# Scores of first and second attention in three fp32r passes, and the last product in column halves

## What is computed

```python
def sliding_window_sink_attention(q, k, v, sinks):          # "first attention"
    ...
    s = jnp.einsum('bnqkgd,bnskd->bnkgqs', qb, kb).astype(jnp.float32) * scale
    ...
    m = jnp.maximum(jnp.max(s, axis=-1, keepdims=True), sink)
    p = jnp.exp(s - m)
...
        sc = jnp.einsum('bqkgd,bskd->bkgqs', qi, ki).astype(jnp.float32) * scale   # windowed_gqa, "second attention"
...
        x = x + jnp.square(jax.nn.relu(h2 @ w_up[l])) @ w_down[l]                  # the last product
    return rms_norm(x, norm_final)
```

## Time and profile before

| | |
|---|---|
| median of 3 runs | 1072.89 us (1072.5 to 1072.98) |
| the profiled execution | 1072.29 us |
| its span, first to last instruction | 1070.5 us |
| mean granted TensorE clock | 0.998 of 2.4 GHz |
| TensorE matmul busy | 1061.8 us, 99% |
| VectorE, ScalarE, GpSimd busy | 797.9, 567.5, 162.4 us |

### The profile page before, as it was taken

One profiled execution on the slowest core, in us unless ns is written; L12 is line 12 of the kernel. 1 busy time (PEld: TensorE's weight loads), 2 busy tenths in 40 slices (PEclk: granted clock), 3 DMA queues, 4 the chain that ended last, 5 costly groups with the idle time before them and its releaser, 6 DMA issues.

```text
span 1070.5 us, 14582 instructions
## 1 busy us (share of the span) xinstructions
PE 1061.8 (99%) x5220; PEld 857.5 (80%) x5220; DVE 797.9 (75%) x1339; ACT 567.5 (53%) x965; POOL 162.4 (15%) x261
## 2 busy tenths in 40 slices
PE   9999999999999999999999999999999999999997
PEld 7787787887777788767778889988888888888886
DVE  7888887867888865376556669975795886796795
ACT  6766766556676544254354437644453443443455
POOL 2000000120665421022134310012000000000003
PEclk9999999999999999999999999999999999999999
DMA  6422232332121233222423235334704503503301
GB/s 232 143 73 89 93 95 92 118 118 89 41 80 40 80 99 107 91 62 77 137 81 99 79 124 152 102 119 146 264 0 142 193 1 118 197 0 114 141 1 79
DMA packets 35960, 109.97 MB, mean 103 GB/s; under 512 B 4016, under 2 KB 9008, under 8 KB 35888
## 3 DMA queue, kind: packets, MB, share of 16 engines
q1 hardware_dynamic: 34880, 106.09, 29.5%
q0 software_dynamic: 576, 2.10, 1.1%
q10 hardware_dynamic: 432, 0.86, 0.2%
HBM read 103.26 MB, written 2.10 MB: 98 GB/s over the span
## 4 chain that ended last, share of the span: by engine, by line
PE 95%; DVE 1%; ACT 1%; SPq 1%; DMA 1%; issue 0%; DVEq 0%; ACTq 0%
PE ps L1139 23%; PE ps L1141 23%; PE ps L1140 23%; PE ps L1076 5%; PE ps L1077 5%; PE ps L1078 5%; PE ps L1229 2%; PE ps L1309 2%; PE ps L1273 2%; PE ps L1095 1%; PE ps L1096 1%; PE ps L1097 1%; SPq L917 1%; PE ps L1303 1%; PE ps L1025 1%; PE ps L1243 1%
## 5 line engine op out<-in xcount | busy, mean ns | idle before, releaser
L1139 PE MATMUL ps<-xgh,wh 128*128 128x512 f32 x783 | 309.9, 396 | 0.8 <-DVE xgl L1796 0.5
L1141 PE MATMUL ps<-xgh,wl 128*128 128x512 f32 x783 | 305.2, 390 | 0.0
L1140 PE MATMUL ps<-xgl,wh 128*128 128x512 f32 x783 | 305.0, 389 | 0.0
L1738 DVE TENSOR_TENSOR wl<-raw,wh 128x1024 fp32r<-128x1024 f32 x144 | 180.6, 1255 | 38.1 <-ACT wh L1349 36.5
L1349 ACT ACTIVATE wh<-raw 128x1024 fp32r<-128x1024 f32 x144 | 150.8, 1050 | 74.9 <-PE ps L1141 53.6
L1139 PEld LDWEIGHTS ps<-xgh,wh 128*128 128x128 f32 x783 | 147.0, 188 | 36.4 <-issue 7.2
L1141 PEld LDWEIGHTS ps<-xgh,wl 128*128 128x128 f32 x783 | 147.0, 188 | 31.4
L1140 PEld LDWEIGHTS ps<-xgl,wh 128*128 128x128 f32 x783 | 147.1, 188 | 29.5 <-issue 0.2
L1554 ACT ACTIVATE Pt<-Pt,stat 128x256 f32<-128x256 f32 (+2 forms) x128 | 64.3, 503 | 89.9 <-DVE stat L2014 34.8
L1076 PE MATMUL ps<-wh,fh 128*128 128x512 f32 x224 | 87.1, 389 | 0.0
L1077 PE MATMUL ps<-wl,fh 128*128 128x512 f32 x224 | 87.1, 389 | 0.0
(11 more groups left out here) (294 smaller groups left out, 1918.2 us busy)
## 6 DMA issues: line engine op xcount, KB each, us to landing
raw<-wst SPq DMA_DIRECT2D x144, 512.0 KB, 3.5
b<-wdn SPq DMA_DIRECT2D x32, 512.0 KB, 6.8
bst<-nbias SPq DMA_DIRECT2D x8, 256.0 KB, 3.5
xtok<-xblk SPq DMA_DIRECT2D x16, 128.0 KB, 2.5
gx<-xT SPq DMA_DIRECT2D x3, 512.0 KB, 6.6
outT<-xtok SPq DMA_DIRECT2D x3, 512.0 KB, 2.6
Vb<-vblk SPq DMA_DIRECT2D x16, 64.0 KB, 2.0
wt<-woc SPq DMA_DIRECT2D x2, 512.0 KB, 4.7
```

Source lines behind the costliest of these rows:

```text
L1139: e.matmul(o, high, a, start=(k == 0), stop=False)
L1140: e.matmul(o, high, b, start=False, stop=False)
L1141: done = e.matmul(o, low, a, start=False, stop=stop)
L1738: e.tensor_tensor(wl_t[:, v % NHL, :], src, f32(wh_t[:, v % NHL, :]), ALU.subtract).then_inc(lo_done, 1)
```

## The change

Scores. `sink_scores` and `window_scores` take the place of the float32 matmul of L1229. Each runs three fp32r passes in place of one float32 matmul. The high parts are ScalarE copies, the low parts VectorE subtractions: of the keys once, of the queries chunk by chunk. The key copies `ke` and `kea` go; in their place the keys' two parts are swapped between the halves of the partitions by four DMAs each (`ksh2`, `ksl2`, `kah2`, `kal2`). The parts of the queries need room and get it where tensors lie that are written later: first attention's in the place of `sgt` (chunks 0 to 3) and of the upper half of `y2h` and `y2l` (chunks 4 to 7), second attention's in the place of `yah` and `yal`. So the first write of `sgt` waits for the 32nd score. `qa` shrinks to two buffers.

Last product. The twelve 512 column matmuls of the last product become 24 of 256 columns, first all of the left column half, into a PSUM bank of its own (6), then the right half. The left half of what bank 1 held is added before; the left half of the last product is added and squared while TensorE is at the right half, and the last square and the last add are 256 columns wide. Its weight units' places are set for the new order.

```diff
@@ class Chunks, downs
             for i in range(8):
-                self.unit_of.append((len(self.units) + i // 2 % 2, 2 * (i // 4) + i % 2))
-            self.units += [(("form", r, "P4", 0), t, t + 5), (("form", r, "P4", 1), t + 2, t + 7)]
+                self.unit_of.append((len(self.units) + (i // 2 if i < 4 else i) % 2, i % 4))
+            self.units += [(("form", r, "P4", 0), t, t + 6), (("form", r, "P4", 1), t + 2, t + 7)]
@@ SyncE, swaps
-                q.wait_ge(qn_done, 1)
-                e.dma_start(ke[1][lo, :], qu[0][hi, :]).then_inc(swap_in, 16)
-                e.dma_start(ke[0][hi, :], qu[0][lo, :]).then_inc(swap_in, 16)
...
+                q.wait_ge(ksh_done, 1)
+                e.dma_start(f32(ksh2[lo, :]), f32(ksh[hi, :])).then_inc(swap_in, 16)
+                e.dma_start(f32(ksh2[hi, :]), f32(ksh[lo, :])).then_inc(swap_in, 16)
+                q.wait_ge(ksl_done, 1)
+                e.dma_start(f32(ksl2[lo, :]), f32(ksl[hi, :])).then_inc(swap_in, 16)
+                e.dma_start(f32(ksl2[hi, :]), f32(ksl[lo, :])).then_inc(swap_in, 16)
...
@@ TensorE
+            def last_down_tile(name, i, v):
...
+                if i == 0:
+                    q.wait_ge(ev_done, ev_no(("up", FINAL, 5)))
+                    q.wait_ge(quarter_done, 1)
+                o = bank[(LAST_BANK, ch.bank[name])[i // 2]][:, 256 * (i // 2):256 * (i // 2) + 256]
+                for k in (2 * (i % 2), 2 * (i % 2) + 1):
...
+                    e.matmul(o, a, wh_t[:, v % NHL, w], start=(k == 0 and i == 0), stop=False, skip_group_check=True)
+                    e.matmul(o, a, wl_t[:, v % NHL, w], start=False, stop=False, skip_group_check=True)
+                    done = e.matmul(o, b, wh_t[:, v % NHL, w], start=False, stop=(k == KH - 1), skip_group_check=True)
...
+            def sink_scores(m, i, a, job):
+
+                g = job["g"]
+                q.wait_ge(q1h_done, 4 * g + a + 1)
+                q.wait_ge(q1l_done, 4 * g + a + 1)
...
+                q.wait_ge(swap_in, 64)
+                q.wait_ge(qn_done, 3 + 4 * g + 2 * job["half"])
+                for n, (own, seen) in enumerate(((q1h[g], (ksh, ksh2)), (q1l[g], (ksh, ksh2)), (q1h[g], (ksl, ksl2)))):
+                    for p, r in ((0, lo), (1, hi)):
+                        done = e.matmul(score_place(m, i + p), own[r, a, blk(job["n"])], seen[p != g][r, keys(job)],
+                                        start=(n == 0), stop=(n == 2))
+                        if n == 2:
+                            done.then_inc(score_done, 1)
+
+            def window_scores(m, i, a, job):
...
@@ ScalarE
+            def sink_key_high():
+                yield sum_tick(0) + 3.8
+                q.wait_ge(qn_done, 1)
+                q.wait_ge(tile_done, A_END)
+                e.activation(ksh, qu[0], ACT.Copy).then_inc(ksh_done, 1)
+
+            def sink_query_highs():
+                for c in range(8):
+                    yield sum_tick(c + 1) + (2.8 if c == 3 else 3.7)
+                    q.wait_ge(qn_done, c + 2)
+                    q.wait_ge(tile_done, A_END if c < 4 else end["kv", 1] + 1)
+                    e.activation(q1h[c // 4][:, c % 4, :], q1[:, c, :], ACT.Copy).then_inc(q1h_done, 1)
...
@@ VectorE
-            def key_copies():
...
+            def key_low():
+                yield sum_tick(0) + 4.6
+                q.wait_ge(ksh_done, 1)
+                e.tensor_tensor(ksl, qu[0], f32(ksh), ALU.subtract).then_inc(ksl_done, 1)
+
+            def query_lows():
+                for c in range(8):
+                    yield sum_tick(c + 1) + (3.4 if c == 3 else 4.3)
+                    q.wait_ge(q1h_done, c + 1)
+                    e.tensor_tensor(q1l[c // 4][:, c % 4, :], q1[:, c, :], f32(q1h[c // 4][:, c % 4, :]), ALU.subtract).then_inc(q1l_done, 1)
...
+                q.wait_ge(score_done, 32)
                 e.scalar_tensor_tensor(sgt[:, c, :], th_b[c % 2], 1.0, gu_b[c % 2], ALU.add, ALU.mult).then_inc(silu2_done, 1)
...
+                if name == LAST:
+                    e.tensor_tensor(x_[:, 256:512], done_[:, 256:512], x_[:, 256:512], ALU.add).then_inc(ev_done, 1)
...
+            def first_quarter():
...
+                yield ev_at[LAST] - 2.2
+                q.wait_ge(tile_done, end[LAST] - 1)
+                q.wait_ge(quarter_done, 1)
+                e.tensor_tensor(x_, bank[LAST_BANK][:, 0:256], x_, ALU.add).then_inc(quarter_done, 1)
```

More of the change, by code:

```diff
@@ L382, in build @@
         q1 = sb("q1", [128, KD, S], F, ph)
-        ke = [sb(f"ke{g}", [128, S], F, ph)[:, :] for g in range(2)]
+        ksh, ksh2 = (sb(n, [128, S], R, ph)[:, :] for n in ("ksh", "ksh2"))
         V1 = sb("V1", [128, NBLK, 128], F, ph)
+        qs = ExitStack()
+        q1h0, q1l0 = (sb(n, [128, 4, S], R, qs) for n in ("q1h0", "q1l0"))
+        qs.close()
+        q1h, q1l = (q1h0, q1h1), (q1l0, q1l1)
         sgt = sb("sgt", [128, KD, S], F, ph)
@@ L392, in build @@
         sql = [sb(f"sql{i}", [128, S], R, ph)[:, :] for i in range(2)]
+        ksl2 = sb("ksl2", [128, S], R, ph)[:, :]
         ph.close()
         ph, qk, ma, vp = ExitStack(), ExitStack(), ExitStack(), ExitStack()
+        qs = ExitStack()
+        qah, qal = (sb(n, [128, 4, S], R, qs) for n in ("qah", "qal"))
+        qs.close()
         yah = sb("yah", [128, 4, S], R, ph)
@@ L828, in build @@
         FINAL = ROUNDS - 1
+        LAST, LAST_BANK = ("dn", FINAL, "P4", 1), 6
         def form_ready(q, name):
@@ L1216, in scores @@
                             continue
[L1217 to L1222, removed]
-                                own, seen = q1[r, 4 * g + a, blk(job["n"])], ke[g][r, keys(job)]
-                            else:
-                                q.wait_ge(ev_done, ev_no(("z", 3)))
-                                q.wait_ge(ka_done, 2)
-                                q.wait_ge(swap_in, 64)
-                                own, seen = qa[r, a, blk(job["n"])], kea[r, job["g"], keys(job)]
-                            e.matmul(score_place(m, i + p), own, seen, start=True, stop=True).then_inc(score_done, 1)
+                        if kind == "w":
+                            window_scores(m, i, a, job)
+                            continue
@@ new lines, in window_scores @@
+            def window_scores(m, i, a, job):
+                q.wait_ge(qah_done, a + 1)
+                q.wait_ge(qal_done, a + 1)
+                q.wait_ge(kah_done, 1)
+                q.wait_ge(kal_done, 1)
+                q.wait_ge(swap_in, 128)
+                for n, (own, seen) in enumerate(((qah, (kah, kah2)), (qal, (kah, kah2)), (qah, (kal, kal2)))):
+                    for p, r in ((0, lo), (1, hi)):
+                        done = e.matmul(score_place(m, i + p), own[r, a, blk(job["n"])], seen[p != job["g"]][r, keys(job)],
+                                        start=(n == 0), stop=(n == 2))
+                        if n == 2:
+                            done.then_inc(score_done, 1)
@@ L2330, in downs @@
                 q.wait_ge(ev_done, ch.added[name])
-                x_ = acc_(ADDS_TO[p], s)
-                e.tensor_tensor(x_, bank[ch.bank[name]], x_, ALU.add).then_inc(ev_done, 1)
+                x_, done_ = acc_(ADDS_TO[p], s), bank[ch.bank[name]]
+                if name == LAST:
+                    e.tensor_tensor(x_[:, 256:512], done_[:, 256:512], x_[:, 256:512], ALU.add).then_inc(ev_done, 1)
+                else:
+                    e.tensor_tensor(x_, done_, x_, ALU.add).then_inc(ev_done, 1)
+            def first_quarter():
+                x_ = acc_(ADDS_TO["P4"], 1)[:, 0:256]
+                yield ev_at["dn", FINAL, "P7", 1] + 1.0
+                q.wait_ge(tile_done, end["dn", FINAL, "P7", 1] + 1)
+                q.wait_ge(ev_done, ch.added[LAST])
+                e.tensor_tensor(x_, bank[ch.bank[LAST]][:, 0:256], x_, ALU.add).then_inc(quarter_done, 1)
+                yield ev_at[LAST] - 2.2
+                q.wait_ge(tile_done, end[LAST] - 1)
+                q.wait_ge(quarter_done, 1)
+                e.tensor_tensor(x_, bank[LAST_BANK][:, 0:256], x_, ALU.add).then_inc(quarter_done, 1)
             def row_outs():
```

101 lines of the change are left out of this document (72 added, 29 removed).

## The result

| | before | after |
|---|---|---|
| median, 9 runs each | 1072.82 us (1072.35 to 1073.71) | 1075.52 us (1075.03 to 1077.1) |
| the profiled execution | 1072.29 us | 1075.73 us |
| its span | 1070.5 us | 1073.9 us |

The ratio of the runs is 1.0026, 95% interval 1.0017 to 1.0034. The change makes the kernel 2.7 us slower. The forecast was 1071.4 us, the range 1069.2 to 1074.6.

The account below looks back on a forecast made before the run. The prediction took TensorE, busy 99% of the span, to bound the kernel. Scores -3.23, stalls +1.75, Vb chain +0.25 and tail -0.27 summed to -1.5 us, forecast 1071.4 us, range 1069.2 to 1074.6.

Parts of the forecast that it names:

- Scores: First and second attention's scores on TensorE: three fp32r passes replace one float32 matmul, -3.23 us, bounds -3.9 and -2.6.
- The narrow job: First attention's four 128 key score jobs: 0.76 us each for 0.65, taken as +0.10 each.
- Rival 3: Narrow passes run at their stream, by the back-to-back gap rule: 1070.7 us, chance 0.10.
- Stalls in first attention: TensorE waits around the query splits at four places without cover: +1.75 us, bounds 0 and 5.6.
- The first three: Stalls at the third head chunk (about 0.3 us), the fifth head chunk (0.5) and before job 1 (0.5).
- The fourth: Stall at job 9: the last query's high part stands behind an exponential on ScalarE, 0.45 us.
- Jobs 2 to 8 don't wait longer: First attention: low parts fall behind the last bias the next job needs, or where VectorE waits for TensorE: no added wait.
- The Vb chain: Second attention: savings of jobs 22 and 23's half jobs return as waiting for Vb rows, +0.25 us, bounds 0 and 0.35.
- The tail: Kernel's end: column halves add 0.20 us on TensorE, last add and square save 0.47: -0.27, bounds -0.45 and +0.1.
- rival 2: The waits around first attention's splits aren't there: -3.3 us, 1069.6 us, chance 0.26.
- the cheap narrow price: Narrow score jobs at their stream's pace, 4 x 0.18 us less than forecast; with rival 2 the range's lower end.
- Rival 5: All eight queries' splits in a row between head norm and TensorE's next wait, 11.2 us: 1080.8 us, chance 0.10.

Follow-up runs that it names:

- e9: Changed kernel, nothing moved, GpSimd's low parts of the squares of head chunks 6 and 8 cut to 64 of 512 columns: 1074.44 us (1.0014).
- e2: Kernel before with second attention's split scores alone: 1071.13 us (0.9986).
- e7: Changed kernel with six of first attention's eight query splits left out, the fifth's low part placed as in e4: 1071.28 us (0.9984).
- e11: Changed kernel with thirteen steps at other places in the engines' orders, the moves of e5 among them: 1070.12 us (0.9972).
- e8: Changed kernel with 18 more small matmuls ahead of TensorE's warm-up at the kernel's start: 1083.45 us, one execution.
- e1: Kernel before with first attention's split scores alone: 1077.13 us (1.0042).
- e4: Changed kernel with the fifth and seventh query's low parts moved behind the biases in VectorE's order: 1074.16 us (1.0018).
- e5: As e4, with the eighth query's norm, high part and low part moved earlier: 1072.91 us (1.0005).

## Why the prediction was wrong

- **Scores.** Forecast -3.23 us, found -2.8. Two thirds of the difference are the narrow jobs, the rest some 0.01 us in each of the others. Wide, double and half jobs came out within 0.02 us of the forecast: 0.91, 1.62, 0.55, 0.72 (the last double has a break of 0.25 in it, counted below). The narrow job was mis-sized: 0.76 forecast, 0.81 found, +0.17 each instead of +0.10. The inner pairs start 0.11 us apart, as I said, but the outer two don't run at their stream of 0.064: the first takes 0.16, the last 0.20 until the next work. The Trainium skill's price for a weight load (TensorE: Matmul & The Clock Gate, section LDWEIGHTS), 107 ns, agrees with those 0.11. The 56 ns of its section Back-to-back issue gap isn't reached by any pair here; the section gives that figure for a matmul by itself, and says that it under-counts where each matmul has a weight load. Rival 3 is out.
- **Stalls in first attention.** Forecast 1.75 us, found 4.5 between the two traces (the seven waits of the table, 4.3, and the break of 0.25, whose cause no run shows), and this is the step that failed. The first three were right: 0.26, 0.45 and 0.36 us for 0.3, 0.5 and 0.5. The fourth was too small: I let job 9 wait for one exponential (0.45), but the high part also waits behind ScalarE's order from job 8 on, and it was 0.3 + 1.25. The sentence "Jobs 2 to 8 don't wait longer" was false: 0.68 at the eighth head sum, ahead of job 7, and 1.0 before job 8. I had priced the low parts of the fifth and the seventh query at the 0.69 of the earlier trace rows, where GpSimd is idle; beside GpSimd they took 1.62 and 1.79. e9 shows that this is the cause: with nothing moved and GpSimd's two instructions made short, both waits are gone. That GpSimd makes the squares' low parts from the fifth query chunk on stood in my own text on the kernel, and the trace of before had such a collision, seen from GpSimd, around the weight low part that VectorE starts at 302.83 (the same two GpSimd instructions take 0.72 elsewhere):

```profile
302.43 1.78 POOL L2436 TENSOR_SCALAR Pt<-Pt,stat 128x128 f32<-128x128 f32 x2 [0.32 <-DVE stat L2042]
```

- **The Vb chain.** Forecast +0.25 us, found +1.4: 0.3 as I said (e2 shows it alone), the rest one long issue. Which issue a fetch falls on couldn't be read from the trace of before, but that 16 issues of 0.60 us in a row are on the path, and that anything which holds one of them is paid in full, could.
- **The tail.** Forecast -0.27, found -0.25 between the traces.
- **The sum.** 3.9 - 1.6 + 1.4 - 0.25 = 3.4 us between the profiled executions, as measured; the forecast had 0.3 - 1.75 + 0.25 - 0.27 = -1.5. In the 3.9 some 0.5 are in no single wait of the table: 0.05 stood there before the third head sum, behind each of the three waits at a head sum the second matmul comes another 0.07 to 0.09 late (0.31 us after the first instead of 0.23 or 0.24), and the rest is in smaller pieces. The recorded range had a slip at its other end: rival 2 with the cheap narrow price is 1068.9 us, not 1069.2.
- **Rival 5** named the right engines and the right direction, but not the mechanism: not eight splits in a row. Its deciding point was a mean of 0.67 us a query; the six that e7 leaves out cost 0.7 each. Its chance of 0.10 was too low, as the case against it was argued from ticks and one slack, and not from the last wait of each job.

## What to carry to other kernels

Where an instruction with two inputs in SBUF is added to VectorE, put GpSimd's timeline beside it before you take its price from a row where GpSimd was idle. And a collision is not always paid where it is seen: look at what the delayed engine hands on, and when TensorE comes for it. With VectorE 75% busy, what an added step costs is set by its place among the steps that TensorE waits for: the same splits cost TensorE 5.1 us in one order and 0.8 in another (e11). And a change with parts in different stages is best measured part by part: here two parts gained and one lost more than both.

## What the runs showed of the hardware

- A VectorE subtraction and a GpSimd subtraction, both with two inputs in SBUF, ran one after the other where they met: 0.69 became 1.62 and 1.79 us on the one, 1.29 became 1.76 on the other, depending on who starts first; with GpSimd's instruction cut to 64 columns (0.32 us) VectorE's fell to 0.69 and 0.82 (e9).
- A fetch of 16 KB of code on queue 8 that falls among back to back DMA issues of SyncE makes one of them last 1.1 to 1.7 us instead of 0.60, in eight traces of eight. With the fetch 3.4 us ahead of the run, the run takes its usual 10.41 us (e8). What in the chip ties the two together no run shows.
- With new weights of 64 rows by 128 columns for each, pairs of fp32r matmuls start 0.11 us apart with 128 moving columns and 0.12 with 256, and float32 pairs, of which a score needs two, 0.11 and 0.22. So three passes instead of one lose on 128 keys (0.65 became 0.81 us) and gain on 256 (1.06 became 0.91).
- In e8 the granted clock was 0.54 on average in the three microseconds from 330, mostly the 1.2 GHz level, with matmuls 0.43 us apart instead of 0.23; it cost 1.6 us. TensorE had stood for 1.25 us in the middle of job 9 before it. The same stand in the traces of after, e1, e4 and e9 had no such stretch behind it, so the cause is open. The executions without a trace say a little more. The longer ones of e4 and e9 have a mean granted clock of 0.997 or 0.998, the shorter ones mostly 0.999 or 1.000; one of after's nine is longer by as much (1077.1 us at 0.997); of e5, in which this stand is gone, none is under 0.999. A stretch such as e8's takes 1.6 us and, by my estimate, 0.0016 off the mean clock, so it fits, but only e8's trace shows one. The row of the windows view (window, its length, busy time and count of PE, PEld, DVE, ACT, POOL, then the granted clock):

```profile
330.00:333.00 3.00, 3.00 (x10) 2.40 (x9) 3.00 (x8) 1.51 (x5) 0.57 (x2) 0.54 0.14 18
```
